# Two transformer blocks on one core: outputs stored in packed pairs of rows, the first weight tile issued first, memory's root one step later

## What is computed

```python
# first block: differential attention and pooling, gated; then a squared-ReLU MLP
h = rmsnorm(x, norm_attn_g); q, k, v, pool, gates = split(h @ w_in)
lam = exp(sum(lam_q1 * lam_k1)) - exp(sum(lam_q2 * lam_k2)) + lambda_init
a = rmsnorm((softmax(q1 k1) - lam * softmax(q2 k2)) @ v, subln_g) * (1 - lambda_init)
x = x + (sigmoid(g_a) * a + sigmoid(g_p) * pooled) @ w_out
x = x + square(relu(rmsnorm(x, g) @ w_up)) @ w_down
x = rmsnorm(x, final_norm_g)
# second block: stick-breaking attention and convolution, gated
x = x + merged @ w_mix_out
# attention over 256 memory tokens
x = x + cross_attention(rms_norm(x, g_q), rms_norm(mem, g_kv), w_q, w_kv) @ w_o
# gated MLP, then the last norm
x = x + (silu(gate) * up) @ w_ffn_out
return rms_norm(x, norm_final)
```

## Time and profile before

| | us |
|---|---|
| median of three executions | 1583.36 |
| the profiled execution, its own time | 1583.8 |
| its span, first to last instruction | 1582.0 |
| TensorE busy in it | 1569.1 |
| VectorE, ScalarE (ACT), GpSimd (POOL) busy | 916.0, 636.8, 81.9 |

### The profile page before, as it was taken

The page is one execution under the profiler, slowest core; times in us unless marked ns, Lnnn a source line. Parts: engine busy times, 40 slices in busy tenths (PEclk is TensorE's granted clock), DMA queues, the critical chain, the costliest instruction groups (busy, mean ns, idle before and its releaser), DMA issues.

```text
span 1582.0 us, 19023 instructions
## 1 busy us (share of the span) xinstructions
PE 1569.1 (99%) x7374; PEld 1294.4 (82%) x7374; DVE 916.0 (58%) x1353; ACT 636.8 (40%) x994; POOL 81.9 (5%) x66
## 2 busy tenths in 40 slices
PE   9999999999999999999999999999999999999997
PEld 7877777788888888888887888898888888888886
DVE  7776878666645445357787435455655544434435
ACT  5455767643222222255445344353444232222212
POOL 3000000020000000040000010010001000000002
PEclk9999999999999999999999999999999999999999
DMA  5333232333233323233221242344132322332322
GB/s 202 112 102 100 81 96 72 107 130 97 93 107 93 94 93 107 89 97 98 67 68 59 74 137 83 113 133 134 58 97 95 109 94 94 96 104 94 99 82 74
DMA packets 49674, 155.64 MB, mean 98 GB/s; under 512 B 6192, under 2 KB 9136, under 8 KB 49456
## 3 DMA queue, kind: packets, MB, share of 16 engines
q1 hardware_dynamic: 49136, 153.85, 30.9%
q10 hardware_dynamic: 448, 0.57, 0.1%
HBM read 148.11 MB, written 2.10 MB: 95 GB/s over the span
## 4 chain that ended last, share of the span: by engine, by line
PE 97%; DVE 1%; ACT 1%; DMA 1%; issue 0%; ACTq 0%; DVEq 0%
PE G L966 84%; PE SC L966 4%; PE O L966 2%; PE TP L966 2%; PE M L966 2%; PE TP L1315 1%; PE TP L1261 1%; DVE X L2392 0%; DMA QK<-T 0%; DMA RAW<-in_va 0%; ACT WH L1403 0%; DVE WL L1864 0%; PE TP L1365 0%; ACT L1400 0%; DVE MGl L1864 0%
## 5 line engine op out<-in xcount | busy, mean ns | idle before, releaser
L966 PE MATMUL G<-XGh,WH 128*128 128x512 f32 x1248 | 493.4, 395 | 0.0
L966 PE MATMUL G<-XGh,WL 128*128 128x512 f32 x1248 | 486.2, 390 | 0.0
L966 PE MATMUL G<-XGl,WH 128*128 128x512 f32 x1248 | 486.2, 390 | 0.0
L1864 DVE TENSOR_TENSOR WL<-RAW,WH 128x1024 fp32r<-128x1024 f32 (+3 forms) x281 | 339.1, 1207 | 192.8 <-ACT WH L1403 192.4
L1403 ACT ACTIVATE WH<-RAW 128x1024 fp32r<-128x1024 f32 (+3 forms) x281 | 283.8, 1011 | 185.2 <-PE G L966 174.0
L966 PEld LDWEIGHTS G<-XGh,WH 128*128 128x128 f32 x1248 | 234.3, 188 | 55.2 <-issue 6.5
L966 PEld LDWEIGHTS G<-XGh,WL 128*128 128x128 f32 x1248 | 234.2, 188 | 49.5
L966 PEld LDWEIGHTS G<-XGl,WH 128*128 128x128 f32 x1248 | 234.5, 188 | 46.8 <-issue 0.2
L966 PE MATMUL G<-MGh,WH 128*128 128x512 f32 x400 | 156.5, 391 | 0.9 <-ACT T L1742 0.6
L966 PE MATMUL G<-MGl,WH 128*128 128x512 f32 x400 | 155.7, 389 | 0.0
L966 PE MATMUL G<-MGh,WL 128*128 128x512 f32 x400 | 155.6, 389 | 0.0
(11 more groups left out here) (315 smaller groups left out, 1796.1 us busy)
## 6 DMA issues: line engine op xcount, KB each, us to landing
RAW<-in_up SPq DMA_DIRECT2D x32, 512.0 KB, 3.5
RAW<-in_dn SPq DMA_DIRECT2D x32, 512.0 KB, 3.5
RAW<-in_fg SPq DMA_DIRECT2D x22, 512.0 KB, 3.5
RAW<-in_fu SPq DMA_DIRECT2D x22, 512.0 KB, 3.6
RAW<-in_g SPq DMA_DIRECT2D x16, 512.0 KB, 3.6
RAW<-in_f SPq DMA_DIRECT2D x16, 512.0 KB, 3.5
X<-in_x SPq DMA_DIRECT2D x16, 256.0 KB, 4.1
RAW<-in_q SPq DMA_DIRECT2D x8, 512.0 KB, 3.7
```

Of the source, the lines that this page charges most:

```text
L966: return e.matmul(dst, st, mv, start=start, stop=stop, skip_group_check=True)
L1864: return e.tensor_tensor(dst, src, hi.bitcast(F32), ALU.subtract)
```

## The change

- Start. The gains are issued by SP behind x's first tile instead of by ACT, whose queue now begins with the first weight tile. One warming matmul fewer.
- Lambda's product stands ahead of the scaling of gains; the sum on TensorE comes in the fourth weight tile, behind its first token block. The scaling has a third instruction, the last norm's gain times sqrt(128).
- Memory's norm is 17 ticks behind the load instead of 16: behind gate (4, 1) and the matmuls of branch (4, 1).
- The refinement of the memory queries' root is a step of its own, behind key tile 5.
- End. A new ACT step `scaled` multiplies each row of X by its gain in place: rows 0 to 3 whole behind half 0 of tile 6, halves of rows 4 to 7 behind half 0 of tile 7, and in half 1 behind each tile's square, the last one behind the root's Exp. The root's Ln reads the sum's bank itself, with scale and bias; VectorE's mean waits for the Ln and runs beside Exp. `out` covers two rows in one VectorE pass of 512 columns, X times RB, into a packed tile (T for half 0, RAW for half 1), and SP stores it as 256 KB: eight stores instead of sixteen. The output in DRAM is laid out by partition, half and row, and the host puts it back in order. Half 0's outputs stand two behind tile 5, one behind tile 6 and one behind tile 7.

The core of the diff (context cut; where only a slice got a name, it is left out):

```diff
@@ -81,10 +81,14 @@
-WARM = 11
+WARM = 10
 HALVED = 4
+HALVES = (slice(0, MEM), slice(MEM, S))
+ROWS = 2
@@ -249,9 +253,10 @@
         self.put("ones")
-        self.put("gains")
             self.put("x0", k)
+            if k == 0:
+                self.put("gains")
@@ -266,9 +271,9 @@
             self.put("sq", "attn", k)
+        self.put("lam_prod")
         self.put("half_gains")
-        self.put("lam_prod")
-        self.v_gemm("va", 0, 4, {(2, 3): [("lam",)], (3, 2): [("norm", "attn")]})
+        self.v_gemm("va", 0, 4, {(3, 0): [("lam",)], (3, 2): [("norm", "attn")]})
@@ -487,7 +492,7 @@
             self.later(20 + k, "mem_split", k)
-        self.later(16, "norm", "mem")
+        self.later(17, "norm", "mem")
@@ -508,6 +513,8 @@
                 self.put("norm", "mq")
+            elif n == 5:
+                self.put("newton", "mq")
@@ -560,6 +567,8 @@
         self.put("sq_half", n, half)
+        if half == 1 and n < 7:
+            self.put("scaled", n, 1)
@@ -583,19 +592,22 @@
             self.put("sq", "fin", n)
+        scaled = {6: (0, 1, 2, 3), 7: (4, 5, 6, 7)}
             self.half_gemm(n, 0)
+            for m in scaled.get(n, ()):
+                self.put("scaled", m, 0)
+        beside = {4: [("norm_half", 0), ("mean", 0), ("refine", 0)], 5: [("out", 0, 0), ("out", 2, 0)],
+                  6: [("out", 4, 0)], 7: [("out", 6, 0)]}
             self.half_gemm(n, 1)
-            if n == HALVED:
-                self.put("norm_half", 0)
-            elif n < 7:
-                for j in range(3):
-                    self.put("out", 3 * (n - HALVED - 1) + j, 0)
-        self.put("out", 6, 0)
-        self.put("out", 7, 0)
+            for step in beside[n]:
+                self.put(*step)
         self.put("norm_half", 1)
-        for n in range(8):
+        self.put("scaled", 7, 1)
+        self.put("mean", 1)
+        self.put("refine", 1)
+        for n in range(0, 8, ROWS):
@@ -758,6 +770,7 @@
         LASTh, LASTl = (QK[:, w, :, :].rearrange("p a s -> p (a s)") for w in range(2))
+        PACKED = (T[:, :, :].rearrange("p a s -> p (a s)"), RAW[:, :, :].rearrange("p a s -> p (a s)"))
@@ -879,6 +892,13 @@
         OUT = tally("out")
+        gained = sem("gained")
+        SCALED = tally("scaled")
+        def outputs(n, half):
+            at = slice(n * MEM, (n + ROWS) * MEM)
+            return PACKED[half][:, at], out[:, half, at]
@@ -894,7 +914,9 @@
                 kind, arg = step[0], step[1:]
-                if kind == "x0":
+                if kind == "gains":
+                    e.dma_start(GN[:, :], a["gains"]).then_inc(d_gain, 16)
+                elif kind == "x0":
@@ -955,10 +977,10 @@
                 elif kind == "out":
-                    n, hs = arg[0], slice(arg[1] * MEM, (arg[1] + 1) * MEM)
+                    packed, result = outputs(*arg)
                     e.wait_ge(out_done, OUT[step])
-                    e.dma_start(out[n][:, hs], X[:, n, hs]).then_inc(d_out, 16)
-            e.wait_ge(d_out, 16 * 16)
+                    e.dma_start(result, packed).then_inc(d_out, 16)
+            e.wait_ge(d_out, 8 * 16)
@@ -1117,7 +1139,7 @@
                     u, g, half = arg
-                    hs = slice(half * MEM, (half + 1) * MEM)
+                    hs, bank = HALVES[half], G[:, g % 2, 0:MEM]
@@ -1125,14 +1147,14 @@
                         c = slice(k * P, (k + 1) * P)
-                        mm(G[:, g % 2, 0:MEM], wh[:, c], MGh[:, k, hs], start=(k == 0))
-                        mm(G[:, g % 2, 0:MEM], wh[:, c], MGl[:, k, hs])
-                        t = mm(G[:, g % 2, 0:MEM], wl[:, c], MGh[:, k, hs], stop=(k == 5))
+                        mm(bank, wh[:, c], MGh[:, k, hs], start=(k == 0))
+                        mm(bank, wh[:, c], MGl[:, k, hs])
+                        t = mm(bank, wl[:, c], MGh[:, k, hs], stop=(k == 5))
                     half = arg[0]
...
@@ -1413,10 +1435,7 @@
                 kind, arg = step[0], step[1:]
-                if kind == "gains":
-                    e.dma_start(GN[:, :], a["gains"]).then_inc(d_gain, 16)
-                elif kind == "load" and arg[0] == 0:
+                if kind == "load" and arg[0] == 0:
@@ -1810,7 +1829,7 @@
                     n, half = arg
...
@@ -1818,9 +1837,23 @@
+                elif kind == "scaled":
+                    n, half = arg
+                    hs = HALVES[half] if n >= HALVED else slice(0, S)
+                    if (n, half) == (0, 0):
+                        e.wait_ge(half_gain, 3)
+                    if n < HALVED:
+                        e.wait_ge(sq_done, SQN["sq", "fin", n])
+                    else:
+                        e.wait_ge(fh_sq, HALF["sq_half", n, half])
+                    hi(X[:, n, hs], X[:, n, hs], gain(G_OUT, n)).then_inc(gained, 1)
                 elif kind == "norm_half":
-                    hs = slice(arg[0] * MEM, (arg[0] + 1) * MEM)
-                    root(T[:, 6, hs], RB[:, hs], NRM[step])
+                    hs = HALVES[arg[0]]
+                    e.wait_ge(sum_done, SUM[step])
+                    e.activation(RB[:, hs], M[:, hs], ACT.Ln, bias=EPSC, scale=P / D).then_inc(ln_done, 1)
+                    e.wait_ge(ln_done, NRM[step])
+                    e.activation(RB[:, hs], RB[:, hs], ACT.Exp, scale=-0.5).then_inc(r_exp, 1)
@@ -1849,7 +1882,7 @@
                     n, half = arg
...
@@ -1912,6 +1945,8 @@
                     e.tensor_scalar(GN[:, c:c + 8], GN[:, c:c + 8], 0.5, None, ALU.mult).then_inc(half_gain, 1)
+                    c = G_OUT
+                    e.tensor_scalar(GN[:, c:c + 8], GN[:, c:c + 8], math.sqrt(P), None, ALU.mult).then_inc(half_gain, 1)
@@ -1958,12 +1993,22 @@
                     e.tensor_scalar(ms, norm_bank(arg[0])[:, 0:n], 1.0 / D, EPS, ALU.mult, ALU.add).then_inc(ms_done, 1)
+                    if arg[0] != "mq":
+                        refine(ms, r, tmp)
+                elif kind == "newton":
+                    r, ms, tmp = NORM[arg[0]]
+                    e.wait_ge(ms_done, NRM["norm", arg[0]])
                     refine(ms, r, tmp)
-                elif kind == "norm_half":
-                    hs = slice(arg[0] * MEM, (arg[0] + 1) * MEM)
-                    e.wait_ge(sum_done, SUM[step])
-                    e.tensor_scalar(T[:, 6, hs], M[:, hs], 1.0 / D, EPS, ALU.mult, ALU.add).then_inc(ms_done, 1)
+                elif kind == "mean":
+                    hs = HALVES[arg[0]]
+                    e.wait_ge(ln_done, NRM["norm_half", arg[0]])
+                    e.tensor_scalar(T[:, 6, hs], M[:, hs], P / D, P * EPS, ALU.mult, ALU.add).then_inc(ms_done, 1)
+                elif kind == "refine":
+                    hs = HALVES[arg[0]]
+                    e.wait_ge(ms_done, NRM["norm_half", arg[0]])
                     refine(T[:, 6, hs], RB[:, hs], T[:, 7, hs])
@@ -2377,21 +2422,24 @@
                     n, half = arg
...
                         e.wait_ge(unit_done, gemm_done(step))
-                    e.tensor_tensor(X[:, n, hs], X[:, n, hs], G[:, turn_of[step] % 2, 0:MEM], ALU.add).then_inc(g_empty, 1)
+                    e.tensor_tensor(X[:, n, hs], X[:, n, hs], G[:, turn_of[step] % 2, 0:MEM],
+                                    ALU.add).then_inc(g_empty, 1)
                     n, half = arg
-                    hs = slice(half * MEM, (half + 1) * MEM)
+                    hs, k = HALVES[half], ROWS
                         e.wait_ge(r_done, NRM["norm_half", half])
-                    e.scalar_tensor_tensor(X[:, n, hs], X[:, n, hs], gain(G_OUT, n), RB[:, hs], ALU.mult,
-                                           ALU.mult).then_inc(out_done, 1)
+                    last = n + k - 1
+                    e.wait_ge(gained, SCALED["scaled", last, half if last >= HALVED else 0])
+                    r = RB[:, hs].unsqueeze(1).to_broadcast([P, k, MEM])
+                    packed = outputs(n, half)[0].rearrange("p (a s) -> p a s", a=k)
+                    e.tensor_tensor(packed, X[:, n:n + k, hs], r, ALU.mult).then_inc(out_done, 1)
@@ -2470,7 +2518,8 @@
         aps[name] = nc.dram_tensor(f"in_{name}", v.shape, mybir.dt.from_np(v.dtype), kind="ExternalInput").ap()
-    out = nc.dram_tensor("out_0", (8, P, S), F32, kind="ExternalOutput").ap()
+    out = nc.dram_tensor("out_0", (P, 2, 8 * MEM), F32, kind="ExternalOutput").ap()
     r = _run(nc, [arrays], core_ids=[0])
-    return np.ascontiguousarray(r.results[0]["out_0"].reshape(D, S).T).reshape(1, S, D)
+    y = np.asarray(r.results[0]["out_0"]).reshape(P, 2, 8, MEM)
+    return np.ascontiguousarray(y.transpose(1, 3, 2, 0)).reshape(1, S, D)
```

8 lines of the change are left out of this document (4 added, 4 removed).

## The result

The changed kernel takes 1581.55 us (median of 20 runs, 1581.01 to 1582.74); the kernel before takes 1584.53 in 20 runs of its own (1583.33 to 1586.53), 1.17 more than the median of three that the prediction started from. The ratio is 0.9981, its 95% interval 0.9975 to 0.9987: 2.98 us less, or 0.19%, where 3.12 were forecast. The profiled execution took 1581.2 with a span of 1579.4; before it was 1583.8 and 1582.0. The two profiles are thus 2.6 apart.

A forecast was written before the change was run, and what follows sets the result against it. TensorE was taken as the bound, busy 1569.1 of 1582.0 us, leaving some 13 us. Terms 0.45 + 0.18 + 0.72 + 0.69 + 1.08 = 3.12 us, from a median of 1583.36 to 1580.2; range 1579.3 to 1581.0.

The forecast's parts named there:

- Start, 0.45: First matmul: weights issued 0.45 us earlier with the gains moved to SP, so the first product starts at 5.52.
- the point from which the prediction counted a loss: Attention norm: if GpSimd's sum of squares slid past 26.7 us, each further us would be lost.
- A rival had late gains and a late tile: Start does not move: gains behind more of x, or second weight tile late; 0.45 lost, 1580.7 us; chance 0.14.
- Lambda, 0.18: Lambda's sum near 22.6 us: TensorE's wait for VectorE's lambda product goes, saving 0.18 us (0 to 0.4).
- Memory's root, 0.72: Gate beside memory's root, 954 us: gate evacuated before the root's table load, saving 0.72 us (0.3 to 0.75).
- refinement, 0.69: Eighth key tile, 1071 us: refinement moved behind tile 5's low half, so the stall goes, saving 0.69 us (0.2 to 0.7).
- the margin at the first value tile: Behind the moved refinement: value tile's remainder done at 1073.5, its product due at 1073.75, so 0.25 us of margin.
- End, 1.08: Root, outputs and stores: last store issued 1.73 us earlier, less 0.65 for larger stores' landing; saves 1.08 (0.8 to 1.5).
- the last issue: SP's last store issue: at 1578.04 instead of 1579.77 us, 1.73 earlier, as SP keeps up with four DMAs.
- Stores become the bound: Rival at the end: four 256 KB stores below 333 GB/s land as late as now; 1581.3 us; chance 0.14.
- The best end of the range: Best ends summed: 0.65 + 0.2 + 0.75 + 0.7 + 1.5 = 3.8 us, and what overlaps: 1579.2.
- The prediction put the 1.18 down to two SBUF inputs: Gains scaling on VectorE, 1.18 us beside GpSimd's additions: said to agree with the two-SBUF-input lockout rule.

The follow-up runs named there:

- a_scores_later: The changed kernel with the first block's attention, and all that follows it, one tick later in the order; median 1580.84 us, ratio 0.9973 to the kernel before.
- b_memory: The kernel before with only memory's root one tick later and the memory queries' refinement one tile later; 1583.1 us, ratio 0.9989.
- c_first_small: a_scores_later with the second half's first two outputs as single rows, the others in pairs; median 1581.4 us, ratio 0.9979 to the kernel before.
- b_end: The kernel before with only the end changed (root from PSUM, gains multiplied in ahead, outputs in pairs of rows); 1583.67 us, ratio 0.9994.

## Why the prediction was right, and where not

**The sum.** 3.12 forecast, 2.98 between the medians. The time itself, 1580.2, is 1.35 below the measured 1581.55, of which 1.17 is the starting point: three runs of the kernel before gave 1583.36, twenty give 1584.53. That the sum is so near is in part luck, as its errors cancel. In the profiled pair the start is 0.45 short, memory gave 0.36 and the end 0.3 more than forecast.

**Start, 0.45: failed.** The failing step is the landing of the gains. I had them land 0.45 later or more, at 4.55, and ready 0.48 ahead of need. They landed at 4.6 to 5.2 in the new place, 3.4 to 4.0 after their issue instead of 3.1 to 3.3, and are now the last thing the first product waits for (in five of six executions with the new start; in `a_scores_later` it came at 5.34, right behind the warming). The weights did gain what I took: their copy on ScalarE starts at 4.4 to 5.0 instead of 5.0 to 5.5. Of 0.45, 0.19 is won in the profiled pair and 0.30 in the mean. The rest goes further on. The prediction moved x's tiles by one issue, 0.42; the eighth landed 0.8 later in the profiled pair, and in four of six executions ScalarE waited for the second. GpSimd's additions end at 26.6 to 27.3, around or past 26.7, the point from which the prediction counted a loss; the profiled pair shows 0.20 of it, all that had been won. A rival had late gains and a late tile (of weights, not of x) cost the whole 0.45, and I gave it too small a chance.

**Lambda, 0.18: 0.14 in the pair,** of which 0.03 had come before its place (the last product ahead of it in the old order is already 0.22 ahead). Right as a mechanism. In `b_memory` the same old order cost 0.84 of waiting, so the edit is also worth something in executions in which VectorE comes late.

**Memory's root, 0.72: 0.95; refinement, 0.69: 0.82.** The mechanisms are as told, and the margin at the first value tile held (0.39 where 0.25 was forecast). Both terms were too small, since I counted only the gap. Behind each gap the next interval is wider as well: 0.33 for 0.23 between 954.61 and 954.94 in the trace of before, 0.22 for 0.12 behind 1071.33. Of the root, a further 0.1 is spread over intervals and is not resolved.

**End, 1.08: 1.2 behind the last sum, and 0.17 ahead of it.** By its terms: the last issue is 1.62 earlier as counted from the last sum (predicted 1.73; the root gave 0.33 of it for 0.46), and from the last issue to the end it is 2.66 instead of 2.23, so 0.43 more where I took 0.65. By the rate in the Trainium skill (DMA: Bandwidth & Descriptors, "Anatomy of one DMA"), whose formula is a fit to DMAs issued by GpSimd, an estimate for the larger store is 0.3 more; these are issued by SyncE, and the measured 0.43 lies between that and mine. "Stores become the bound" did not happen: the engines stood at nine tenths, but `c_first_small`, with an earlier first store, ended later. The 0.17 ahead of the last sum I had not foreseen. `b_end` shows 0.16 at the same place, so it belongs to the end's edits: with pairs VectorE is free when the last product comes.

**What hid the sum in one pair of profiles.** The 0.66 at 91 us is a varying wait, which `b_memory` shows without the change. Without it the two profiles would be 3.3 apart. As that wait alone ran from 0.1 to 1.8, a difference of two single executions is here no better than 1 to 2 us.

**A smaller error.** The best end of the range takes 0.2 for lambda, whose own bound was 0.4, and adds 0.36 for what overlaps without a source.

## What to carry to other kernels

When a load that everything waits for is issued earlier by sending another behind it, the other becomes the one that everything waits for: list all inputs of the first product with their landings, not with their issues, and take several executions. A stall behind a busy engine goes whole when the step that blocks it can stand one tile later, and gives a little more than its gap. At the end, count issues: eight stores issued 0.47 apart were slower than four twice as large, whose landing took only 0.43 longer.

## What the runs showed of the hardware

Small size did not help a DMA at the start: the gains, 42.5 KB, took 3.1 to 3.3 us as the first of their queue, 3.4 to 4.4 as the second, and 6.6 behind all of x, where a store of 256 KB at the end took 2.1. Their place went with x's tiles too: with the gains first on ScalarE's queue x's eighth tile landed at 11.2 to 11.5, with the gains second on SyncE's at 12.0 to 12.8.

A VectorE instruction on 64x2 elements took 1.25 us beside a GpSimd addition and ended with it (at 23.21 and 23.20); two on 128x8 took 0.15 each right behind it. In the trace of before it was the other way round: the 128x8 scaling took 1.18 and ended with the addition (22.50 and 22.46), and the 64x2 instruction behind it took 0.14. The Trainium skill (SBUF — State Buffer, "SBUF: two separate sides") has the two engines lock each other out for whole instructions where VectorE's has two SBUF inputs or runs in a two-port mode. The rows agree: a small instruction pays what is left of the addition. It is not simply the first one that pays, as a 128x1 scaling took 0.14 inside the same addition in the trace of before. The prediction put the 1.18 down to two SBUF inputs, but that scaling has one tile and a constant; what it shows is only that it ended with the addition.

A 256-column Ln read from PSUM took 0.47 us and the next instruction of ScalarE followed at 0.51; from SBUF these were 0.42 and 0.45. The first also had a scale and a bias tile, which the second had not, so the 0.05 is not shown to be PSUM's.
